# A 16-slot weight ring and eight high-part slots for the experts of a two-layer diffusion step on one Trainium2 core

## The reference

```
def expert_choice_ffn(h, w_router, w_g, w_u, w_d):       # h: 640 tokens of 1024
    aff = jax.nn.softmax(xt @ w_router, axis=-1)          # 16 experts
    gate, idx = lax.top_k(aff.T, cap)                     # 80 tokens for each expert (64 + 16)
    xe = xt[idx]
    hg = jnp.einsum("ecd,edf->ecf", xe, w_g)              # 80 x 1024 x 1024
    hu = jnp.einsum("ecd,edf->ecf", xe, w_u)
    y = jnp.einsum("ecf,efd->ecd", jax.nn.silu(hg) * hu, w_d)
    y = y * gate[..., None]
    out = jnp.zeros_like(xt).at[idx.reshape(-1)].add(y.reshape(-1, D))
```

## Time and profile before

| | us |
|---|---|
| median of 3 runs | 3199.35 (3191.02 to 3199.44) |
| time of the profiled execution | 3196.53 |
| its span in the profile | 3194.7 |
| first expert matmul to last, layer 0 | 1024.53 to 1662.2 |
| PE busy | 2808.2 |

### The profile page before, as it was taken

One profiled execution on the slowest core, in us unless ns is written; L12 is line 12 of the kernel. 1 busy time (PEld: TensorE's weight loads), 2 busy tenths in 40 slices (PEclk: granted clock), 3 DMA queues, 4 the chain that ended last, 5 costly groups with the idle time before them and its releaser, 6 DMA issues.

```text
span 3194.7 us, 41275 instructions
## 1 busy us (share of the span) xinstructions
PE 2808.2 (88%) x13702; PEld 2002.4 (63%) x13702; DVE 1987.4 (62%) x3185; ACT 1603.8 (50%) x2382; POOL 855.4 (27%) x513
## 2 busy tenths in 40 slices
PE   6869999999995998998979999999999589898894
PEld 2367777777774555555548777777778355555552
DVE  7853366434355788888875346633434688888885
ACT  5643444333223766666654434323323366666663
POOL 0003000311211444444442000211231244444443
PEclk9989999999995999999999999999998799999997
DMA  9932111211332999999981211211133499999996
GB/s 314 330 122 62 42 34 34 68 38 41 112 111 86 330 333 329 334 327 331 331 315 53 69 31 34 68 39 55 45 117 119 161 331 331 330 331 330 329 332 226
DMA packets 193419, 587.46 MB, mean 184 GB/s; under 512 B 26888, under 2 KB 36934, under 8 KB 193286
## 3 DMA queue, kind: packets, MB, share of 16 engines
q1 hardware_dynamic: 176886, 529.77, 47.3%
q0 software_dynamic: 16336, 55.81, 6.0%
q10 hardware_dynamic: 64, 0.13, 0.0%
HBM read 560.47 MB, written 25.16 MB: 183 GB/s over the span
## 4 chain that ended last, share of the span: by engine, by line
PE 59%; DVE 14%; issue 9%; DMA 9%; ACT 7%; POOL 1%; SPq 0%; ACTq 0%; DVEq 0%; POOLq 0%
PE bank L443 16%; PE bank L445 14%; PE bank L444 14%; DMA ring<-in_w_e_up 6%; PE bank L800 5%; DVE low L1717 4%; PE bank L828 4%; ACT high L1006 4%; PE bank L818 2%; DVE low L1283 2%; ACT bank L1056 1%; DMA ring<-in_w_mod 1%; DVE xeT_low L1288 1%; DVE att L1367 1%; PE bank L628 1%
## 5 line engine op out<-in xcount | busy, mean ns | idle before, releaser
L1006 ACT ACTIVATE high<-ring 128x1024 fp32r<-128x1024 f32 (+1 forms) x1012 | 1048.8, 1051 | 529.2 <-PE bank L445 362.4
L1717 DVE TENSOR_TENSOR low<-ring,high 128x1024 fp32r<-128x1024 f32 (+1 forms) x564 | 836.1, 1514 | 229.5 <-ACT high L1006 228.8
L1886 POOL TENSOR_TENSOR low<-ring,high 128x1024 fp32r<-128x1024 f32 (+1 forms) x194 | 508.2, 2620 | 690.3 <-ACT high L1006 690.3
L443 PE MATMUL bank<-high,hT_high 128*128 128x512 f32 (+2 forms) x1280 | 524.1, 409 | 29.9 <-ACT sigr L1079 12.6
L443 PE MATMUL bank<-high,xeT_high 128*80 128x512 f32 x1024 | 423.2, 413 | 105.1 <-DVE xeT_low L1288 62.6
L445 PE MATMUL bank<-high,hT_low 128*128 128x512 f32 (+2 forms) x1280 | 486.3, 380 | 0.0
L444 PE MATMUL bank<-low,hT_high 128*128 128x512 f32 (+2 forms) x1280 | 485.7, 379 | 0.0
L444 PE MATMUL bank<-low,xeT_high 128*80 128x512 f32 x1024 | 412.8, 403 | 0.0
L445 PE MATMUL bank<-high,xeT_low 128*80 128x512 f32 x1024 | 412.3, 403 | 0.0
L1283 DVE TENSOR_TENSOR low<-ring,high 128x1024 fp32r<-128x1024 f32 (+2 forms) x254 | 300.3, 1212 | 110.6 <-ACT high L1006 109.3
L1177 ACT ACTIVATE att<-bank,st 128x640 f32<-128x640 f32 (+3 forms) x200 | 137.0, 685 | 400.9 <-DVE st L1549 285.6
(11 more groups left out here) (240 smaller groups left out, 3585.1 us busy)
## 6 DMA issues: line engine op xcount, KB each, us to landing
ring<-in_w_e_down SPq DMA_DIRECT2D x260, 512.0 KB, 4.8
ring<-in_w_e_gate SPq DMA_DIRECT2D x256, 512.0 KB, 6.0
ring<-in_w_e_up SPq DMA_DIRECT2D x256, 512.0 KB, 7.0
ring<-in_w_mod SPq DMA_DIRECT2D x96, 512.0 KB, 6.0
ring<-in_w_gate SPq DMA_DIRECT2D x64, 512.0 KB, 4.1
ring<-in_w_in SPq DMA_DIRECT2D x24, 512.0 KB, 4.5
ring<-in_w_branch SPq DMA_DIRECT2D x16, 512.0 KB, 3.7
ring<-in_w_out SPq DMA_DIRECT2D x16, 512.0 KB, 5.2
```

Source lines behind the costliest of these rows:

```text
L443: nc.tensor.matmul(out, lhs[0], rhs_high, start=start, stop=False)
L1006: A(high[:, g % HIGH, :, 0:w], ring[:, g % RING, :, 0:w], ACT.Copy).then_inc(high_done, 1)
L1717: V.tensor_tensor(low[:, (g + HIGH) % RING, :, 0:w], ring[:, (g + HIGH) % RING, :, 0:w], high[:, g % HIGH, :, 0:w].bitcast(F32), ALU.subtr ...
L1886: G.tensor_tensor(low[:, g % RING, :, 0:w], ring[:, g % RING, :, 0:w], high[:, g % HIGH, :, 0:w].bitcast(F32), ALU.subtract).then_inc(low_ ...
```

## The change

The experts get 16 ring slots and 8 high slots. The eight new ring slots lie in the attention's work area `att`, and four new high slots lie in `hT_high`, the transposed activations. Attention, gates and `w_out` keep 8 and 4. `plan_ring()` writes down for each chunk its slot, the fill count and what it has to wait for. The first five expert chunks go to slots 8 to 12 (`SLOT_E`), behind the end of the attention units (`o_ev`); the slots 13 to 15 wait until the normed rows have been transposed and stored. The looped part is cut at another place (two experts are 48 chunks, three rounds of 16 slots), with the same order of matrices. DVE and ACT handle chunk j + 8 at position j where they handled j + 4; their side tasks keep their positions. The splits of the next layer's first four chunks stand at j = 8 to 11 of the last down stage, and the four extra chunks after the last layer are gone.

```
@@
+RING_E = 16
+HIGH_E = 8
+SLOT_E = [8, 9, 10, 11, 12, 0, 1, 2, 3, 4, 5, 6, 7, 13, 14, 15]
@@
+def plan_ring():
+    slot, fills, free, hslot, hfree = [], [], [], [], []
+    count, last, hlast = [0] * RING_E, [None] * RING_E, [None] * HIGH_E
+    for g in range(N_CHUNKS):
+        e = (g - CH_MOD) % CH_LAYER - CH_DENSE if g >= CH_MOD else -1
+        a, h = (SLOT_E[e % RING_E], e % HIGH_E) if e >= 0 else (g % RING, g % HIGH)
+        count[a] += 1
+        slot.append(a)
+        fills.append(count[a])
+        free.append(None if last[a] is None else last[a] + 1)
+        hslot.append(h)
+        hfree.append(None if hlast[h] is None else hlast[h] + 1)
+        last[a] = hlast[h] = g
+    return slot, fills, free, hslot, hfree
@@
-        ring = sb("ring", [P, RING, KC, NW])
-        low = over("low", [P, RING, KC, NW], ring_at, 0)
-        high = sb("high", [P, HIGH, KC, NW], F32R)
-        hT = [sb("hT_high", [P, KD, T * P], F32R), sb("hT_low", [P, KD, T * P], F32R)]
+        sb("ring_mem", [P, RING * KC * NW])
         att_at = nc.sbuf_base
         att = sb("att", [P, 9952])
+        ring = nc.alloc_sbuf_tensor_at("ring", [P, RING_E, KC, NW], F32, offset=(ring_at + 31) // 32 * 32)
+        low = over("low", [P, RING_E, KC, NW], ring_at, 0)
+        high_at = nc.sbuf_base
+        sb("high_mem", [P, HIGH * KC * NW])
+        high = over("high", [P, HIGH_E, KC, NW], high_at, 0)
+        hT = [sb("hT_high", [P, KD, T * P], F32R), sb("hT_low", [P, KD, T * P], F32R)]
@@ SP
+                        if i is None and g == g0 and k == 0:
+                            sp.wait_ge(o_ev, N_UNIT * (l + 1))
+                        if i is None and SLOT[g + k] == 13:
+                            sp.wait_ge(norm_tr, 2 * T * (2 * l + 2))
+                            for b in range(2):
+                                sp.wait_ge(xn_out[b], xn_store(l, 4 - b))
@@
-            for j in range(HIGH):
-                g = N_CHUNKS + j
-                fill(g % RING, w_chunk(w_e_down[L - 1, NE - 1], 0, NW, j), g - RING + 1)
@@ ACT
-                    act.wait_ge(ring_used, i * (2 * CH_EXP) + (g - HIGH + 1))
+                    act.wait_ge(ring_used, i * (2 * CH_EXP) + HIGH_FREE[g])
@@
-                        split_high(g + HIGH, i, NEXT_W if last and l + 1 < L and j >= 4 * NQ - HIGH else NW)
+                        if not last or j < CH_GATE0:
+                            split_high(g + HIGH_E, i)
+                        elif l + 1 < L and j < CH_GATE0 + HIGH:
+                            split_high(chunk_no(l + 1, j - CH_GATE0))
@@ DVE
+                for j in range(HIGH, HIGH_E):
+                    split_low(g0 + j)
                 rows_mod(0, 2 * NE * l, 2 * NE * l)
```

More of the change, by code:

```diff
@@ L368, in hybrid_step @@
         const_in = sem("const_in")
-        ring_full = [sem(f"ring_full{i}") for i in range(RING)]
+        ring_full = [sem(f"ring_full{i}") for i in range(RING_E)]
         ring_used = sem("ring_used")
@@ L499, in _, with fill @@
             sp.dma_start(mask_sw[:, :, :], k_mask_sw).then_inc(const_in, 16)
[L501 to L505, removed]
+            def fill(g, src, width=NW):
+                if SLOT_FREE[g] is not None:
+                    sp.wait_ge(ring_used, SLOT_FREE[g])
+                sp.dma_start(ring[:, SLOT[g], :, 0:width], src).then_inc(ring_full[SLOT[g]], 16)
             for g in range(CH_MOD):
@@ L701, in dense @@
                         ins = three(bank_use(r, 0, w), [t[:, kk, m * P:(m + 1) * P] for t in left],
-                                    high[:, g % HIGH, k, 0:w], low[:, g % RING, k, 0:w], kk == 0, kk == n - 1)
+                                    high[:, HSLOT[g], k, 0:w], low[:, SLOT[g], k, 0:w], kk == 0, kk == n - 1)
                     if m == T - 1:
@@ L892, in w_out_tile @@
                             ins = three(bank(4 + r % 4), [t[:, kk, m * P:(m + 1) * P] for t in mergedT],
-                                        high[:, g % HIGH, k, :], low[:, g % RING, k, :], kk == 0, kk == KD - 1)
+                                        high[:, HSLOT[g], k, :], low[:, SLOT[g], k, :], kk == 0, kk == KD - 1)
                         if m == T - 1:
@@ L946, in matrix @@
                         for half in range(2):
-                            ins = three(bank(first + half)[0:CAP, :], stat(k), high[:, (g + k) % HIGH, half, :],
-                                        low[:, (g + k) % RING, half, :], k == 0, k == KD - 1)
+                            ins = three(bank(first + half)[0:CAP, :], stat(k), high[:, HSLOT[g + k], half, :],
+                                        low[:, SLOT[g + k], half, :], k == 0, k == KD - 1)
                         ins.then_inc(ring_used, 1)
@@ L1282, in split_low @@
                 w = width_of(g)
-                V.tensor_tensor(low[:, g % RING, :, 0:w], ring[:, g % RING, :, 0:w], high[:, g % HIGH, :, 0:w].bitcast(F32),
+                V.tensor_tensor(low[:, SLOT[g], :, 0:w], ring[:, SLOT[g], :, 0:w], high[:, HSLOT[g], :, 0:w].bitcast(F32),
                                 ALU.subtract).then_inc(low_dve, 1)
@@ L1713, in expert @@
                                 low_part(hidT[1][:, ks, :], bank(6 + half, 0, 4 * CAP), hidT[0][:, ks, :], hidT_low)
-                        if not by_pool(g + HIGH):
-                            dve.wait_ge(high_done, i * (2 * CH_EXP) + (g + HIGH + 1))
-                            w = NEXT_W if last and l + 1 < L and j >= 4 * NQ - HIGH else NW
-                            V.tensor_tensor(low[:, (g + HIGH) % RING, :, 0:w], ring[:, (g + HIGH) % RING, :, 0:w],
-                                            high[:, g % HIGH, :, 0:w].bitcast(F32), ALU.subtract).then_inc(low_dve, 1)
+                        ahead = g + HIGH_E
+                        if last and j >= CH_GATE0:
+                            if l + 1 < L and j < CH_GATE0 + HIGH:
+                                split_low(chunk_no(l + 1, j - CH_GATE0))
+                        elif not by_pool(ahead):
+                            dve.wait_ge(high_done, i * (2 * CH_EXP) + (ahead + 1))
+                            V.tensor_tensor(low[:, SLOT[ahead], :, :], ring[:, SLOT[ahead], :, :],
+                                            high[:, HSLOT[ahead], :, :].bitcast(F32), ALU.subtract).then_inc(low_dve, 1)
                     dve.wait_ge(gate_set, n_exp + 1)
@@ L1894, in expert @@
                     for j in range(2 * HIGH + HIGH, (4 if last else 6) * NQ + 1, HIGH):
-                        split_low(g0 + at + j, i, NEXT_W if last and l + 1 < L and j == 4 * NQ else NW)
+                        if last and j == 4 * NQ:
+                            if l + 1 < L:
+                                split_low(chunk_no(l + 1, HIGH - 1))
+                        else:
+                            split_low(g0 + at + j, i)
                         if j == 4 * HIGH and rows:
```

57 lines of the change are left out of this document (33 added, 24 removed).

## The result

| | before | after |
|---|---|---|
| median, us | 3195.67 (4 runs, 3191.02 to 3199.44) | 3279.09 (4 runs, 3276.45 to 3281.11) |
| ratio | 1 | 1.0261, 95% interval 1.0249 to 1.0274 |
| span of the profiled execution, us | 3194.7 | 3274.6 |
| a pass of the expert loop, us | 39.97 | 42.51 |
| the last pass of a layer, us | 26.40 | 30.57 |

The kernel is 2.6% slower, 83 us. The forecast of 3196 us was wrong, and so was its range of 3145 to 3228. The two rows on passes are means over 28 passes and over 2, measured from one start of a down stage to the next. They hold almost all of the 79.9 us between the spans: 28 x 2.54 = 71.1, and 2 x 4.17 = 8.3. In experiments 3 and 10 one of the four runs was far slower (4499.85 and 6972.12 us); the medians given for them count it, and without it they are 3100.20 and 3065.88 us.

The account below looks back on a forecast made before the run. Mutually exclusive DVE and POOL low parts were taken to bound the expert pass. Passes -1.5, start +1.6 and end -3.4 gave -3.3 us on 3196.5, so 3193.2; the median 2.8 above made 3196 us, range 3145 to 3228.

Parts of the forecast that it names:

- the up stage: Expert pass: 14.65 us forecast, the middle of 15.0 with POOL's low part first and 14.3 with DVE's first; before 14.59.
- at worst: Expert pass, upper bound: 40.5 us, from 15.0 up, 14.4 gate and 11.1 down; +24 us in all.
- The first: Expert pass, the forecast: DVE's and POOL's low parts exclude each other and hold it at 39.3 to 40.1 us; chance 0.36.
- The second: Expert pass: the late transfer was worth its whole 1.23 us; -37 us, 3160 us in total; chance 0.24.
- The third: Expert pass: all conflicts fall beside side tasks, so PE's pace holds at 37.1 us; -78 us, 3120; chance 0.05.
- The fourth: Expert weights: transfers bind after all, so each layer's eight early chunks are a gain; 3172 us; chance 0.07.
- The fifth: Down stage: the clock falls behind one 2.2 us wait, 1.7 us each in half the passes; +25 us, 3221; chance 0.17.
- The sixth: Up and gate stages: POOL's order costs the full 15.0 and 14.4 us; +24 us, 3220; chance 0.11.
- Gate stage 13.9: Expert pass: gate stage put at 13.9 us, between a lower bound of 12.9 and 14.4.
- Down stage 11.1: Expert pass: PE alone sets the down stage, 11.1 us.
- Start, "+0.8 a layer": First gather of each layer: extra splits run while POOL prepares it, costing 0.8 us a layer, +1.6 in all.
- At the end: After the last matmul: without the extra parts `y_half` and the scatter come sooner, -2.1 us; layer 0 gets -1.3.

Follow-up runs that it names:

- experiment 3: Kernel after with all low parts on DVE, POOL keeping only gathers and scatters: 3101.86 us, ratio 0.9710.
- experiment 10: As experiment 9, but with high and low parts four ahead instead of eight: 3067.27 us, ratio 0.9606.
- experiment 12: Kernel after with one wait added: POOL waits between its two low parts behind the scatter for DVE's third low part: 3203.51 us, ratio 1.0037.
- experiment 2: Kernel after with 16 slots kept, but high and low parts made four chunks ahead instead of eight: 3143.25 us, ratio 0.9847.
- experiment 9: As experiment 8, with `hidT_low` one position earlier, ahead of DVE's last low part in the gate stage: 3033.27 us, ratio 0.9501.
- experiment 1: Kernel after with POOL's low parts put back to their earlier place relative to its gather and scatter: 3165.71 us, ratio 0.9911.
- experiment 7: Kernel after with all low parts on DVE and high and low parts four ahead, 16 slots kept: 3093.73 us, ratio 0.9686.
- experiment 8: As experiment 6, with DVE's low parts of chunks 4 to 7 moved behind the first rows' `rows_low`: 3067.67 us, ratio 0.9610.
- experiment 6: Kernel after with all low parts on DVE and the up stage's side tasks one or two positions earlier: 3075.06 us, ratio 0.9629.
- experiment 4: Kernel after with the up stage's side tasks one or two positions earlier, POOL's order kept: 3164.75 us, ratio 0.9918.

## Why the prediction was wrong

**The step that failed is the up stage.** It went: POOL "is ready for its next low part at about 5.5 to 6.3. If it comes first, DVE's third is blocked to 7.9", and with DVE first, "two low parts in a row to 12.1" only behind it; from both I took 14.65. In either case I had DVE get its turn after at most one of POOL's parts. The trace has POOL first, at 4.9 and not 5.5 to 6.3 (its scatter kept it for 1.15 us, where I had 2.23), and both parts ahead of DVE, which was ready at 6.0 as I had it: DVE blocked to 10.1, `rows_mod` at 11.1, the stage 17.02. Both parts were ready because all high parts are made eight ahead; I had counted them, and not asked who is next when one ends and both engines want to go. Experiment 12 gives DVE the turn that I had assumed: its third low part is blocked to 7.7, `rows_mod` starts at 8.75 and the up stage takes 14.7 us, against 7.9, 9.05 and 15.0 in my case with POOL first, and the kernel is 8 us above my 3196. My bound for a pass "at worst" was 40.5, so the range could not hold what came.

**The rivals.** The first, the exclusion of the two engines' low parts, was the right mechanism: without POOL's parts, the same 16 slots take 3101.86 us (experiment 3). It only cost more than I let it. The second was right about the transfer and mis-sized: 1.77 us a pass and 51 us (experiment 2), against 1.23 and 37; in the kernel after this gain is there and is eaten. The third, PE's pace, is met only in experiment 9, without POOL's low parts and with the side tasks moved; at 34.55 it lies below my 37.1, as I held the side tasks' positions fixed. The fourth, transfers that bind, falls: 383 GB/s in the loop with no wait of PE. The fifth did not happen in the kernel after, whose wait ahead of the down stage is 0.3 to 0.9 us and not "one piece of about 2.2 us"; where that piece exists (experiment 1) the clock falls in 11 of 28 passes, at 1.57 us each against my 1.7. In experiment 12 a wait of 2.1 us stands ahead of 10 of the 28 down stages, and the clock fell in none of them. The sixth had the right culprit, POOL's order, with 15.0 for the stage in place of 17.0.

**The other terms.** Gate stage 13.9: 13.98 here, but 14.35 in the mean of the 28 passes. I had let the lower clock in this stage cost nothing, "where DVE has PE wait anyway"; behind a wait of 5.2 us it covers up to fourteen matmuls, and that is 0.4 us a pass, some 11 us in all. Down stage 11.1: 11.14. Start, "+0.8 a layer": too small. DVE and POOL at the first gather of the kernel after (compare):

```profile
1014.12 3.48 DVE L1323 TENSOR_TENSOR low<-ring,high 128x1024 fp32r<-128x1024 f32 x3
...
1015.05 3.39 POOL L1924 DMA_INDIRECT U<-x_normed,idx_g  x1 [34.11 <-DVE idx_g L1688]
```

The gather's issue took 3.39 us instead of 0.97, and from `idx_g` to the first matmul it took 11.8 us instead of 9.5: +2.3 in layer 0. I had sized it from scatters that ran beside other work, not beside three such operations in a row. The last pass of a layer I had given nothing but its end; it cost +4.2, again behind POOL's pair and a third part of POOL behind it (1685.88 to 1689.13). With POOL's order put back (experiment 1) the last pass takes 26.3 us and not 30.6. On DVE, four low parts that are 4.6 us of work, and POOL's pair:

```profile
1678.90 11.31 DVE L1760 TENSOR_TENSOR low<-ring,high 128x1024 fp32r<-128x1024 f32 x4 [0.16 <-ACT high L1040]
1678.31 5.26 POOL L1932 TENSOR_TENSOR low<-ring,high 128x1024 fp32r<-128x1024 f32 x2
```

At the end `y_half` starts 0.5 us behind the last matmul's start, as I had it, but what follows the last start of a down stage is shorter by only 0.5 us, where I had -2.1.

## What to carry to other kernels

When two engines exclude each other, a deeper buffer for one of them changes more than its slack: it lets several of its operations become ready together, and they may run as one block that the other has to sit out. So ask not only how long an operation blocks, but how many of them will be ready at once and what on the other engine leads to the critical path. And try the plain thing: giving all the work to the faster engine beat sharing it by 50 us here (experiment 2 against 7), and a wait of 1.25 us for the helper was worth 75.

## What the runs showed of the hardware

- Two operations of POOL that read SBUF, back to back, kept out a waiting DVE operation with two SBUF inputs until both were done (5.25 and 5.19 us), though it had been ready for 1.5 us when the second began (1339.24 and 1340.77 in the kernel after). With POOL stopped in between, DVE ran right behind the first (2.82 us, experiment 12). The Trainium skill (SBUF — State Buffer, Who interferes with whom) says that the one that starts first keeps the other out for the whole instruction. The traces agree for one instruction, as in those 2.82 us, and show that in the kernel after the turn did not pass to the one that waited.
- DVE's low parts in a row hold up POOL too. Its gather issue took 0.97 us alone (before, experiments 2, 7 and 8), 3.4 beside three of DVE's low parts (after, experiments 1 and 12) and 4.4 to 4.5 beside four (experiments 3 and 6), and ended each time 0.84 us behind the last of them, in both layers.
- DVE operations that read PSUM ran at their usual 0.42 us beside a low part of POOL (`rows_mod`'s operations at 1320.28, 1320.75 and 1321.34 took 0.43, 0.42 and 0.43 us, with POOL's low part from 1319.98 to 1322.38, experiment 1).
- The granted clock stood at its upper level in the 28 down stages behind waits of 1.0 to 1.1 us (experiments 6 and 8). Behind waits of 2.1 us it fell in 11 of 28 down stages (experiment 1) and in none of 10 (experiment 12), and behind waits of 2.3 in six of 28 (experiment 4).
